# First attention of a two-block network in units of two heads: scores in opposite row halves and two PSUM banks, every second slot, three banks for the tiles

## What is computed

```
s = einsum(q, k_band) * 64 ** -0.5          # a query block of 128 against its own and the block before
s = where(valid, s - slopes * dist, -inf)   # ALiBi, window of 128
m = maximum(max(s), sink)
p = exp(s - m)
denom = sum(p) + exp(sink - m)
o = einsum(p / denom, v_band)
merged = sigmoid(gate_r) * (y_rnn @ w_o_rnn) + sigmoid(gate_a) * (o @ w_o_attn)
mix = merged @ w_out
```

## Time and profile before

| | |
|---|---|
| runs | 2487.68, 2486.25, 2487.15 us; median 2487.15 |
| span of the profiled execution | 2479.4 us (the page gives no other time of that execution) |
| TensorE products busy | 2362.2 us, 95% of the span |
| VectorE busy | 1400.1 us, 56% |
| ScalarE busy | 1011.1 us, 41% |
| chain that ended last, by engine | TensorE 83%, VectorE 7%, ScalarE 5% |
| slots 14 to 47 | from 102.52 to 259.24 us of the span |

### The profile page before, as it was taken

One profiled execution on the slowest core, in us unless ns is written; L12 is line 12 of the kernel. 1 busy time (PEld: TensorE's weight loads), 2 busy tenths in 40 slices (PEclk: granted clock), 3 DMA queues, 4 the chain that ended last, 5 costly groups with the idle time before them and its releaser, 6 DMA issues.

```text
span 2479.4 us, 35681 instructions
## 1 busy us (share of the span) xinstructions
PE 2362.2 (95%) x13360; PEld 1627.6 (66%) x13361; DVE 1400.1 (56%) x2688; ACT 1011.1 (41%) x1858; POOL 74.7 (3%) x125
## 2 busy tenths in 40 slices
PE   6999999999999999999989999999999889998999
PEld 3777854444444444444458888888888777876888
DVE  4688742222322222232257769886786677776785
ACT  3645531111111111111145555654555566674653
POOL 0000000000000000000000000000000111001000
PEclk8999999999999999999999999999999999999999
DMA  8764679999999999999976555555565655552553
GB/s 315 248 217 144 231 304 426 425 426 426 426 425 425 425 425 425 426 426 425 426 258 203 179 179 194 180 187 186 178 194 178 182 137 140 154 149 91 182 183 123
DMA packets 277971, 673.68 MB, mean 272 GB/s; under 512 B 8484, under 2 KB 236111, under 8 KB 244960
## 3 DMA queue, kind: packets, MB, share of 16 engines
q1 hardware_dynamic: 274656, 663.60, 70.6%
q0 software_dynamic: 3200, 8.53, 2.0%
HBM read 670.45 MB, written 1.12 MB: 271 GB/s over the span
## 4 chain that ended last, share of the span: by engine, by line
PE 83%; DVE 7%; ACT 5%; issue 3%; DMA 2%; DVEq 0%; ACTq 0%; SPq 0%
PE PS L371 26%; PE PS L1454 17%; PE PS L372 13%; PE PS L1476 9%; PE PS L1441 5%; PE PS L379 4%; PE PS L1428 2%; PE PS L380 2%; DVE WS L321 2%; DMA RING<-in_moe_w 1%; ACT WS L317 1%; DVE XG L1571 1%; PE PS L759 1%; DMA RAW<-in_w_ada 1%; PE PS L2057 1%
## 5 line engine op out<-in xcount | busy, mean ns | idle before, releaser
L371 PE MATMUL PS<-HN,WS 128*128 128x512 f32 x1952 | 701.6, 403 | 14.9 <-DVE WS L321 9.3
L321 DVE TENSOR_TENSOR WS<-RAW,WS 128x1024 fp32r<-128x1024 f32 (+1 forms) x452 | 540.6, 1204 | 134.1 <-ACT WS L317 128.8
L372 PE MATMUL PS<-HN,WS 128*128 128x256 f32 x1952 | 548.4, 281 | 0.0
L317 ACT ACTIVATE WS<-RAW 128x1024 fp32r<-128x1024 f32 (+1 forms) x452 | 463.1, 1035 | 83.8 <-PE PS L372 69.8
L1454 PE MATMUL PS<-RING,XG 128*64 128x512 f32 x2048 | 447.0, 594 | 12.1 <-DVE XG L1571 11.0
L371 PEld LDWEIGHTS PS<-HN,WS 128*128 128x128 f32 x1952 | 370.9, 190 | 109.0 <-DVE WS L321 11.5
L372 PEld LDWEIGHTS PS<-HN,WS 128*128 128x128 f32 x1952 | 372.4, 191 | 0.3
L1454 PEld LDWEIGHTS PS<-RING,XG 128*64 128x64 f32 x2048 | 148.9, 137 | 295.9 <-issue 292.3
L1577 DVE TENSOR_SCALAR GLU<-PS 128x256 f32<-128x256 f32 x64 | 27.2, 425 | 414.9 <-PE PS L1454 414.9
L371 PE MATMUL PS<-MI,WS 128*128 128x512 f32 x704 | 245.4, 395 | 0.0
L1476 PE MATMUL PS<-RING,AT 128*64 128x512 f32 x1024 | 226.8, 595 | 14.8 <-ACT AT L1350 14.8
(11 more groups left out here) (356 smaller groups left out, 2574.2 us busy)
## 6 DMA issues: line engine op xcount, KB each, us to landing
RING<-in_moe_w SPq DMA_DIRECT2D x192, 2048.0 KB, 22.4
RAW<-in_ffn_w_in SPq DMA_DIRECT2D x88, 1024.0 KB, 5.1
RAW<-in_attn_w_qkv SPq DMA_DIRECT2D x36, 1024.0 KB, 5.1
RAW<-in_ffn_w_out SPq DMA_DIRECT2D x32, 1024.0 KB, 5.0
RAW<-in_w_ada SPq DMA_DIRECT2D x24, 1024.0 KB, 7.8
RAW<-in_w_in SPq DMA_DIRECT2D x22, 1024.0 KB, 5.3
RAW<-in_ffn_w_out SPq DMA_DIRECT2D x16, 768.0 KB, 4.3
RAW<-in_conv_w_in SPq DMA_DIRECT2D x12, 1024.0 KB, 5.2
```

The costliest lines, as they stand in the source:

```text
L317: act_f(split_tile(0, n), raw_tile(n), ACT.Copy).then_inc(hi_done, 1)
L321: vec.tensor_tensor(split_tile(1, n), raw_tile(n), split_tile(0, n).bitcast(f32), ALU.subtract).then_inc(lo_done, 1)
L371: nc.tensor.matmul(both, hi[:, k, :], x2[:, :, kx, :], start=start, stop=False)
L372: ins = nc.tensor.matmul(half, lo[:, k, :], x2[:, 0, kx, :], start=False, stop=stop)
```

## The change

A unit is now a pair of heads p = u // 2 and a block b; there are 16, and unit u starts in slot 14 + 2u (`starting`), so that scores and weighing fall in even slots and keys in odd ones. The two heads' scores go to banks 3 and 4, their transposed weights side by side to bank 6, their outputs to bank 7. VectorE biases each head, then takes one maximum, one minimum, one copy, one sum, one reciprocal and one output scaling for both. Bank 3 is taken from the tiles of the four mixer layers, which get `banks=3`. Buffers are laid out anew in the same space; the second one for transposed weights moves behind the output buffer.

```diff
-        layers += [Layer("win", 44, cols(A["w_in"][0], lambda pair: P * WIN_PART[2 * pair])),
+        layers += [Layer("win", 44, cols(A["w_in"][0], lambda pair: P * WIN_PART[2 * pair]), banks=3),
 (and wor, woa, wout likewise)
     def dense_bank(L, t):
-        return bank[(L.t0 + t) % 4] if L.banks == 4 else bank[t % L.banks]
+        return bank[(L.t0 + t) % L.banks]
-        NU = 2 * HEADS
+        NU = HEADS
+        def starting(s):
+            return (s - FIRST) // 2 if (s - FIRST) % 2 == 0 and 0 <= s - FIRST < 2 * NU else None
             def exp(u):
                 act.wait_ge(sem("a_max"), u + 1)
-                act_f(ES[b][:, 0:n], ES[b][:, 0:n], ACT.Exp, bias=STAT[:, 0, b:b + 1],
-                      accum_out=STAT[:, 1, b:b + 1]).then_inc(sem("a_exp"), 1)
-                act_f(STAT[:, 2, b:b + 1], SINK[:, 0, x:x + 1], ACT.Exp, bias=STAT[:, 0, b:b + 1]).then_inc(sem("a_sink"), 1)
+                for x in range(2):
+                    act_f(ES[b][:, x, :], ES[b][:, x, :], ACT.Exp, bias=ASTAT[:, 0, b, x:x + 1],
+                          accum_out=ASTAT[:, 1, b, x:x + 1]).then_inc(sem("a_exp"), 1)
+                for x in range(2):
+                    act_f(ASTAT[:, 2, b, x:x + 1], SINK[...], ACT.Exp, bias=ASTAT[:, 0, b, x:x + 1]).then_inc(sem("a_sink"), 1)
             def scores(u):
-                nc.tensor.matmul(bank[4][:, 0:n], PROJ[h, Q + x // 2, b * P:(b + 1) * P], KD[h, x // 4, 0:n], start=True,
-                                 stop=True).then_inc(sem("a_scores"), 1)
+                for x in range(2):
+                    h = slice(64 * x, 64 * x + 64)
+                    last = nc.tensor.matmul(bank[3 + x][:, 0:n], PROJ[h, Q + p, b * P:(b + 1) * P], KD[h, p // 2, 0:n],
+                                            start=True, stop=True)
+                last.then_inc(sem("a_scores"), 1)
             def turn_keys(u):
-                pe.wait_ge(sem("a_exp"), u + 1)
-                for kb in range(b + 1):
-                    last = nc.tensor.transpose(bank[6][:, kb * P:(kb + 1) * P], ES[b][:, kb * P:(kb + 1) * P], IDENT)
+                pe.wait_ge(sem("a_exp"), 2 * u + 2)
+                for x in range(2):
+                    for kb in range(b + 1):
+                        j = x * (b + 1) + kb
+                        last = nc.tensor.transpose(bank[6][:, j * P:(j + 1) * P], ES[b][:, x, kb * P:(kb + 1) * P], IDENT)
 (weigh likewise, to bank[7][:, x * HD:(x + 1) * HD])
             def behind(s):      # TensorE
+                if starting(s) is not None:
+                    scores(starting(s))
+                if starting(s - 1) is not None:
+                    turn_keys(starting(s - 1))
+                if starting(s - 2) is not None:
+                    weigh(starting(s - 2))
             def peak(u):
-                STT(ES[b][:, 0:n], DIST[:, S - n:S], slope[x], bank[4][:, 0:n], ALU.mult, ALU.add).then_inc(sem("a_biased"), 1)
-                o.link(vec.tensor_reduce(m, ES[b][:, 0:n], AX.X, ALU.max, negate=True))
-                TTN(m, m, SINK[:, 1, x:x + 1], ALU.min).then_inc(sem("a_max"), 1)
+                for x in range(2):
+                    STT(ES[b][:, x, :], DIST[:, S - n:S], slope[2 * p + x], bank[3 + x][:, 0:n], ALU.mult,
+                        ALU.add).then_inc(sem("a_biased"), 1)
+                dve.wait_ge(sem("a_biased"), 2 * u + 2)
+                o.link(vec.tensor_reduce(m, ES[b][:, :, :], AX.X, ALU.max, negate=True))
+                TTN(m, m, SINK[:, 1, 2 * p:2 * p + 2], ALU.min).then_inc(sem("a_max"), 1)
             def take_weights(u):
-                vec.tensor_copy(ET[b][:, 0:n], bank[6][:, 0:n]).then_inc(sem("a_ET"), 1)
+                vec.tensor_copy(ET[b][:, :], bank[6][:, 0:2 * n]).then_inc(sem("a_ET"), 1)
             def out(u):
-                TS(OT[:, b, x * HD:(x + 1) * HD], bank[7][:, 0:HD], STAT[:, 4, b:b + 1], None, ALU.mult).then_inc(sem("a_out"), 1)
+                TTN(OT[:, b, p * P:(p + 1) * P] as (p x d), bank[7][:, 0:P] as (p x d),
+                    ASTAT[:, 4, b, :] broadcast to [P, 2, HD], ALU.mult).then_inc(sem("a_out"), 1)
```

More of the change, by code:

```diff
@@ L166, in block_program @@
     STAT = r0("STAT", [8, 2])
+    ASTAT = r0("ASTAT", [5, 2, 2])
     QKG = r0("QKG", [6])
@@ L251, in block_program @@
     n = t = 0
-    before_banks = 4
+    before_banks = layers[0].banks if layers else 4
     for L in layers:
@@ L547, in mixer @@
         BDA, BDX = ru("BDA", [DC, P]), ru("BDX", [DC, P])
-        ES = [ru(f"AES{i}", [S]) for i in range(2)]
-        ET = [ru(f"AET{i}", [S]) for i in range(2)]
+        ES = [ru(f"AES{i}", [2, (i + 1) * P]) for i in range(2)]
+        ET = [ru("AET0", [2 * P]), ra("AET1", [2 * S])]
         assert ru.o <= body0
@@ L793, in scores @@
             def scores(u):
[L794 removed]
+                p, b = u // 2, u % 2
                 n = (b + 1) * P
[L796 removed]
                 if u == 0:
@@ L820, in weigh @@
                     pe.wait_ge(sem("a_out"), u)
-                for kb in range(b + 1):
-                    last = nc.tensor.matmul(bank[7][:, 0:HD], ET[b][:, kb * P:(kb + 1) * P],
-                                            VT[:, kb, x // 4 * HD:(x // 4 + 1) * HD], start=kb == 0, stop=kb == b)
+                for x in range(2):
+                    for kb in range(b + 1):
+                        j = x * (b + 1) + kb
+                        last = nc.tensor.matmul(bank[7][:, x * HD:(x + 1) * HD], ET[b][:, j * P:(j + 1) * P],
+                                                VT[:, kb, p // 2 * HD:(p // 2 + 1) * HD], start=kb == 0, stop=kb == b)
                 last.then_inc(sem("a_pv"), 1)
             def turn_out(m):
-                pe.wait_ge(sem("a_out"), 4 * m + 4)
+                pe.wait_ge(sem("a_out"), 2 * m + 2)
                 if m:
@@ L946, in peak @@
                     dve.wait_ge(sem("a_T"), u - 1)
[L947 to L951 removed]
+                m = ASTAT[:, 0, b, :]
+                for x in range(2):
+                    STT(ES[b][:, x, :], DIST[:, S - n:S], slope[2 * p + x], bank[3 + x][:, 0:n], ALU.mult,
[3 more added lines that the diff above has]
+                TTN(m, m, SINK[:, 1, 2 * p:2 * p + 2], ALU.min).then_inc(sem("a_max"), 1)
             def take_weights(u):
@@ L986, in behind @@
                         o.mark(vec.tensor_tensor_scan(XC[:, c, :], T3[:, c, :], T2[:, c, :], 0.0, ALU.mult, ALU.add))
-                if 0 <= s - FIRST - 1 < NU:
-                    take_weights(s - FIRST - 1)
-                if 0 <= s - FIRST - 2 < NU:
-                    out(s - FIRST - 2)
+                if starting(s - 1) is not None:
+                    take_weights(starting(s - 1))
+                if starting(s - 2) is not None:
+                    out(starting(s - 2))
                 if s == 29:
@@ L1063, in ahead @@
             def ahead(s):
-                if 0 <= s - FIRST < NU:
-                    peak(s - FIRST)
+                if starting(s) is not None:
+                    peak(starting(s))
             run_layer(dve, win, lo_tile, work_win, behind, ahead)
```

37 lines of the change are left out of this document (18 added, 19 removed).

## The result

The changed kernel takes **2469.11 us** (median of 4 runs, 2462.56 to 2472.90), the kernel before on the same chip 2487.41 us (4 runs, 2486.25 to 2489.15). The ratio is 0.9931, interval 0.9914 to 0.9948: 0.7% faster, some 17 us. The forecast was 2475.4 us, and 2469.11 lies 3.3 us under the lower end of its range.

The account below looks back on a forecast made before the run. TensorE was taken to bound slots 14 to 47 (156.72 us). Products save 10.6, modulation pieces lose 1.3, waits shrink 2.4: 11.7 us off 2487.15 gives 2475.4 us; range 2472.4 to 2478.5, on to 2481.6 with rivals.

Parts of the forecast that it names:

- Items 1 and 2: In slots 14 to 47, two heads' scores take 0.63 or 0.41 us, like one's; eight weighings 0.86, four 0.42.
- Rival A: The two heads' scores do not overlap: 5.1 us back, 2480.5 us; chance 0.08.
- Item 3: Keys alone in a slot: two transposes 0.20 us, four 0.42; with scores and weighing, 10.6 us saved over eight pairs.
- Item 4: Nine modulation pieces share slots with keys instead of scores: 1.15 us each where it was 1.01, 1.3 us lost.
- Item 5: VectorE and ScalarE: VectorE is relieved by 2.0 us per pair, so waits shrink by 2.4 us to 10.5.
- Item 6: Keys after two heads' maximum and exponentials: 3.7 us needed, 3.9 available; no wait, bounds 0 and 0.5 us per two-block unit.
- Rivals B and D: Keys wait for two-head maximum and exponentials: 4 to 8 us back, chance 0.12; or whole ring late, 2490.6 us, 0.03.
- Item 7: Three banks for tiles, tightest at slot 47: cost nothing, bounds 0 and 1 us.
- Item 8: Everything behind slot 47 starts earlier by what is gained.
- rival C: Stretch shrinks but the gain is given back behind it, at the attention's output projection: 2487 us; chance 0.05.

Follow-up runs that it names:

- both edits undone: Changed kernel with VectorE's instructions head by head again and a unit starting in every slot instead of every second: 2473.89 us.
- copy first: VectorE's copy of the turned weights and output scaling issued ahead of the whole-tensor steps: 2482.64 us in the kernel before, 2468.69 (6 runs) in the changed kernel.
- either pad: Kernel before with an unused buffer ahead of the weight buffers: 2481.94 us with 32 bytes (10 runs), 2486.75 us with 128 bytes (one run).

## Why the prediction was right, and where it was wrong

The kernel is faster, as forecast, in the stage that it named. The forecast is 6.3 us above the median measured, and the range did not reach down to it. The term for the products was nearly right; the term for the waits was far too small. By its steps:

- **Items 1 and 2** (scores, weighing): right. One-block scores with eight weighings 4.33 us (its terms give 4.25), two-block scores with four 4.09 (4.03). Rival A (no overlap) did not come. The run with both heads in one half has it, and it costs the 0.42 and 0.21 us that the rival gave.
- **Item 3** (keys): 2.99 and 3.27 for 3.03 and 3.25. A pair costs 3.38 instead of 3.24 and saves 1.18 instead of 1.32: 9.4 us for 10.6. Entering a group costs a little more than it was given.
- **Item 4** (pieces): 1.14 for 1.15, a loss of 1.2. Beside it the prediction had said that the Trainium skill (TensorEngine Tiling, Key Properties), by which changing the mode drains TensorE, would make this item a small gain. That was counted wrongly. The changes over two slots do fall from five to four, but because scores are entered half as often, which items 1 and 3 hold already. A piece itself adds one change ahead of scores and two between a tile and keys, so the rule gives a loss for it, and the trace agrees: a piece between a tile and keys costs 0.13 to 0.17 us more.
- **Item 5** is the step that failed, by its size. It let the waits shrink by 2.4 us, from 12.9 to 10.5; they went to 6.1. It took VectorE's relief (2.0 us per pair) less TensorE's haste (1.2), 0.8 us per pair, over three pairs' worth of late slots. The run with VectorE head by head splits the 6.8 us. (a) The merged instructions are worth 4.4 us of it (10.5 to 6.1), where the term had 2.4. The relief counts wherever VectorE is late, not as a difference of rates. (b) Pairs in every second slot, with VectorE's instructions head by head, already bring the waits from 12.9 to 10.5. For this the prediction had no term, and that its own figure was also 2.4 is chance. Part of it is the wait of 2.16 us at slot 16, which goes because no unit starts in slot 15; the prediction had expected the square root to meet the next unit instead. It does at slot 17, but there 0.31 us is all that the keys wait for ScalarE once VectorE's order is mended. In slots 18 to 20 the waits fall from 1.8 to 0.5 us. As the stretch of before lies between 155.80 and 156.91 us, so do these 2.4 us between 1.5 and 2.6. What the room between a unit's maximum and its copy gives by itself, at the density of the kernel before, no run shows. (c) The prediction saw the clock in the earlier trace rows and put one more or one less slow stretch into its bounds. The kernel before had two slow tiles, 17 and 34, 4.5 us each for 3.0, and the changed kernel none. That looks like 3.1 of the 12.9 us, but only about 0.9 of it lengthened the stretch, as slots 17 and 34 of the run with 32 bytes more show; the rest hid waits for VectorE. These 0.9 us are part of (b).
- **Item 6** (the keys' new wait): right. Keys wait in one slot, 33, and not for being two heads. Rivals B and D rested on such waits; they did not come. The timeline of VectorE and ScalarE there shows the old cause, a whole-tensor step ahead of the maximum:

```profile
185.13 2.27 DVE L1011 SCALAR_TENSOR_TENSOR T<-T,PROJ 128x2048 f32<-128x2048 f32 x1
187.44 0.42 DVE L419 TENSOR_TENSOR PROJ<-PS,PROJ 128x256 f32<-128x256 f32 x1
...
189.28 0.16 DVE L965 TENSOR_TENSOR ASTAT<-ASTAT,SINK 128x2 f32<-128x2 f32 x1
...
189.47 0.51 ACT L639 ACTIVATE AES<-AES,ASTAT 128x256 f32<-128x256 f32 x1 [3.32 <-DVE ASTAT L965]
...
190.62 0.66 PE L823 MATMUL PS<-SM,AES 128*128 128x128 f32 x4 [1.66 <-ACT AES L639]
```

  The Trainium skill's warning (TensorEngine Tiling, PSUM Bottleneck) that evacuation may become the bound, which stood beside B, does not come true in this kernel. With both edits undone VectorE is the bound of slot 20, busy 5.27 of 5.51 us, but more by the weight split (1.22 us) and the scans (1.27) than by reading banks (about 1.7 us for copy, scaling, tile and scores). That section's advice, to evacuate several tiles of a bank in one instruction, is what the change does with the copy and the output scaling.
- **Item 7** (three banks): right; they cost nothing, as the run with them alone shows. **Item 8**, and rival C: nothing was given back; slots 48 to the experts take 87.7 us in both.
- **Outside the steps**: the 96 bytes of the new buffer sped the experts by 1.7 us, which no step had.

In sum: work 8.2 us (forecast 9.3), waits 6.8 (2.4), experts 1.7 (0). From 2475.4 this takes 3.4 for the stretch and 1.7 for the experts and gives 2470.3, 1.2 above the median measured, which the runs' spread covers. The unknowns' range was too narrow at the lower end: it let the waits shrink by up to 5 us, and they shrank by 6.8. One miss went the other way and hid a little of this: the groups gained 9.4 us and not 10.6.

## What to carry to other kernels

Price TensorE's groups from the step to the next start; that held within 0.1 us per slot. Then look separately at what the new order does to the engines behind it. Here it gained 6.8 us on waits beside 8.2 on products, by merging VectorE's small instructions and by moving the attention's deadlines, one of them away from a long step on ScalarE. An estimate by rates alone misses both. When waits and slow tiles stand side by side, don't add them up: a slow tile can hide a wait, and its removal then brings the wait back. A step moved off one wait usually lands on another, so read the stretch and not the one wait; and where a stage elsewhere spreads by more than the gain, compare windows and not run times.

## What the runs showed of the hardware

- Two 64-row products in opposite halves and banks overlap fully: 0.43 and 0.64 us for two heads, 0.64 and 1.06 in one half.
- A 3-D reduction of 128 by 2 by 256 takes 686 ns, as long as a plain instruction of 512 elements; the scaling with a broadcast factor 284 ns for 128 elements, as one head's of 64 did. The bounds had been 0.55 to 0.84 and 0.28 to 0.42.
- A dense tile behind a wait of TensorE can run almost wholly at the lower level of 1.2 GHz: granted clock 0.61 to 0.63, 4.5 us for 3.0. The same wait does not always bring it. Behind 2.16 or 2.17 us at slot 16 tile 17 was slow in the kernel before, and in it with the copy first, but at 1.00 with three banks and with either pad. Behind 0.88 and 0.35 us in slot 33 tile 34 was slow in the kernel before and at 1.00 with 32 bytes more. In the versions of the changed kernel tiles were slow behind 1.76, 1.92, 2.08, 2.63 and 3.11 us, and at 1.00 behind 1.50, 1.66 and 1.95. So no length of wait found here decides it.
- The stream of expert weights, 183 pieces of 2 MB, takes 903.5 us with the buffers at one place and 901.6 to 901.8 with them 32, 96 or 128 bytes on. No alignment to 64 or 128 bytes explains it.
